# A macaron encoder block in split fp32: six of eight chunk pairs of the up stages by block products, with weight sums on GpSimd and the gated product kept in DRAM

## What is computed

```
def swiglu(h, w_gate, w_up, w_down):
    return (jax.nn.silu(h @ w_gate) * (h @ w_up)) @ w_down

h = swiglu(rmsnorm(x, pre_g), w_gate, w_up, w_down)     # w_gate, w_up 2048 x 5632; w_down 5632 x 2048
x = x + 0.5 * rmsnorm(h, post_g)
```

## Time and profile before

| | us |
|---|---|
| median of 3 runs | 1826.41 (1826.05 to 1826.48) |
| profiled execution, its own time | 1826.47 |
| its span, first to last instruction | 1824.7 |
| TensorE busy | 1799.3 (99%) |
| VectorE busy | 1300.0 (71%) |
| ScalarE busy | 896.5 (49%) |
| GpSimd busy | 53.2 (3%) |
| mean granted clock of TensorE | 0.996 |

### The profile page before, as it was taken

How to read it: one execution, slowest core, us unless ns; L and a number is a source line. 1 busy time by engine, 2 the same in 40 slices (tenths; PEclk the granted TensorE clock), 3 DMA queues, 4 the chain that set the end, 5 groups by cost and what they waited for, 6 DMA issues and landing times.

```text
span 1824.7 us, 20137 instructions
## 1 busy us (share of the span) xinstructions
PE 1799.3 (99%) x8226; PEld 1493.4 (82%) x8226; DVE 1300.0 (71%) x1333; ACT 896.5 (49%) x1003; POOL 53.2 (3%) x111
## 2 busy tenths in 40 slices
PE   7899999999999999999999999999999999999998
PEld 6788888888888888888888887888888888888886
DVE  4788888888865544765754547888889888755544
ACT  3655455455644433654234446545555555644432
POOL 0000000000000000170000000000000000000000
PEclk9999999999999999999999999999999999999999
DMA  7466666666666566665443665666666666665563
GB/s 254 127 196 194 210 196 189 211 200 193 199 211 193 197 193 191 196 186 171 134 142 117 209 194 162 193 210 197 196 197 197 195 198 205 217 193 192 195 196 128
DMA packets 150652, 345.36 MB, mean 189 GB/s; under 512 B 10568, under 2 KB 11152, under 8 KB 150176
## 3 DMA queue, kind: packets, MB, share of 16 engines
q1 hardware_dynamic: 149712, 339.79, 59.2%
q0 software_dynamic: 736, 4.26, 0.7%
q10 hardware_dynamic: 112, 0.03, 0.0%
HBM read 341.94 MB, written 2.10 MB: 189 GB/s over the span
## 4 chain that ended last, share of the span: by engine, by line
PE 95%; DVE 2%; ACT 1%; issue 1%; DMA 0%; DVEq 0%; POOLq 0%; POOL 0%; ACTq 0%
PE ps L1152 25%; PE ps L1154 25%; PE ps L1153 25%; PE ps L1346 5%; PE ps L1348 5%; PE ps L1347 5%; PE ps L1457 1%; PE ps L1301 1%; DVE wlo L716 1%; ACT xT_hi L438 0%; ACT whi L380 0%; PE ps L1494 0%; ACT xT_hi L418 0%; DVE xT_lo L779 0%; PE ps L1286 0%
## 5 line engine op out<-in xcount | busy, mean ns | idle before, releaser
L716 DVE TENSOR_TENSOR wlo<-raw,whi 128x1024 fp32r<-128x1024 f32 x520 | 626.5, 1225 | 345.7 <-ACT whi L380 343.8
L380 ACT ACTIVATE whi<-raw 128x1024 fp32r<-128x1024 f32 x520 | 542.1, 1058 | 526.1 <-DMA raw<-in_ffn_w_down_dram 241.6
L1152 PE MATMUL ps<-whi,xT_hi 128*128 128x512 f32 x1248 | 494.1, 396 | 15.1 <-DVE wlo L716 13.9
L1154 PE MATMUL ps<-whi,xT_lo 128*128 128x512 f32 x1248 | 487.8, 391 | 0.0
L1153 PE MATMUL ps<-wlo,xT_hi 128*128 128x512 f32 x1248 | 487.2, 390 | 0.0
L1152 PE MATMUL ps<-whi,hT_hi 128*128 128x512 f32 x832 | 324.2, 390 | 0.0
L1154 PE MATMUL ps<-whi,hT_lo 128*128 128x512 f32 x832 | 323.8, 389 | 0.0
L1153 PE MATMUL ps<-wlo,hT_hi 128*128 128x512 f32 x832 | 323.7, 389 | 0.0
L1152 PEld LDWEIGHTS ps<-whi,xT_hi 128*128 128x128 f32 x1248 | 235.2, 188 | 68.6 <-issue 17.0
L1154 PEld LDWEIGHTS ps<-whi,xT_lo 128*128 128x128 f32 x1248 | 235.1, 188 | 49.9
L1153 PEld LDWEIGHTS ps<-wlo,xT_hi 128*128 128x128 f32 x1248 | 235.4, 189 | 46.6
(11 more groups left out here) (154 smaller groups left out, 1661.1 us busy)
## 6 DMA issues: line engine op xcount, KB each, us to landing
raw<-in_ffn_w_down_dram SPq DMA_DIRECT2D x176, 512.0 KB, 4.6
raw<-in_ffn_w_gate_dram SPq DMA_DIRECT2D x116, 512.0 KB, 3.7
raw<-in_ffn_w_up_dram SPq DMA_DIRECT2D x116, 512.0 KB, 3.6
raw<-in_w_in_dram SPq DMA_DIRECT2D x80, 512.0 KB, 3.6
raw<-in_w_out_dram SPq DMA_DIRECT2D x32, 512.0 KB, 4.1
srawB<-in_ffn_w_up_dram SPq DMA_DIRECT2D x30, 512.0 KB, 3.8
srawB<-in_ffn_w_gate_dram SPq DMA_DIRECT2D x30, 512.0 KB, 4.7
srawA<-in_ffn_w_up_dram SPq DMA_DIRECT2D x30, 512.0 KB, 3.8
```

The lines of the kernel that those rows point to most:

```text
L380: nc.scalar.activation(whi[:, slot(g), :], raw[:, slot(g), :], ACT.Copy).then_inc(hi_ready, 1)
L716: V.tensor_tensor(wlo[:, slot(g), :], raw[:, slot(g), :], whi[:, slot(g), :].bitcast(f32), ALU.subtract).then_inc(lo_ready, 1)
L1152: mm(bank, a_hi, whi[:, s, c0:c0 + NT], start=start, stop=False, skip_group_check=skip)
L1154: return mm(bank, a_lo, whi[:, s, c0:c0 + NT], start=False, stop=stop, skip_group_check=skip)
```

## The change

- `NS = 6`, `PLAIN = 2`: six pairs of a tile by block products, two plain.
- The four blocks of a pair are loaded into one of two staging buffers `stg`. The sums are made by **GpSimd** (`weight_sums`) from there into one of three areas `sraw` (`area(q) = (q + 1) % 3`). The hi and lo parts of the raw blocks are made from `stg`, those of the sums from `sraw`, with semaphores of their own (`s_bhi`, `s_blo`, `s_thi`, `s_tlo`).
- GpSimd also makes the token sums (`token_sums`, in two parts of three pairs), and in each tile the lo part of one of the four plain halves (`by_pool`, `plain_lo`).
- The ring for plain halves in tiles 1 to 10 has 2 slots (4 before).
- The gated product no longer goes to `hT` in SBUF: SP stores it to DRAM tile by tile (`store_h`) and loads it back in the down stage (`load_h`), where TensorE transposes it (`hidden`) and ScalarE and VectorE make hi and lo straight from PSUM.
- The orders of all engines in `first_tile`, `up_tile`, `up` and `down` are new. In the first FFN's first tile the transposes of x are made one step earlier.

```diff
-PAIRS = (0, 1, 2)
-PLAIN = 5
-NS = len(PAIRS)
+NS = 6
+PLAIN = KC // 2 - NS
...
+RING_ORDER = (6, 5, 2, 3, 7, 0, 1, 4)
...
+def by_pool(g):
+    return any(b + 16 <= g < d and (g - b) % (2 * PLAIN) == 2 for b, d in ((U1, D1), (U2, D2)))
...
 def area(q):
-    return (q + 1) % 2
+    return (q + 1) % 3
...
+    stg = [at("stg0", 22, [P, 4, NT]), at("stg1", 54, [P, 4, NT])]
...
                 def sums(j, s):
                     q = NS * (j - 1) + s
-                    a = area(q)
+                    dst = stg[q % 2]
                     if q >= 2:
-                        sp.wait_ge(p_done, 7 * (NQ * f + q - 1))
-                    elif q == 1:
-                        sp.wait_ge(w_used, b + 12)
+                        sp.wait_ge(s_t, NQ * f + q - 1)
+                        sp.wait_ge(s_blo, NQ * f + q - 1)
+                    else:
+                        sp.wait_ge(w_used, b + 5)
+                    sp.dma_start(dst[:, 0:2, :], part(1, s, j)).then_inc(s_in[q % 2], 16)
+                    sp.dma_start(dst[:, 2:4, :], part(0, s, j)).then_inc(s_in[q % 2], 16)
...
                 for j in range(1, FTILES):
-                    plain(j, 2)
-                    sums(j, 2)
-                    plain(j, 3)
+                    sums(j, 3)
+                    sums(j, 4)
+                    sums(j, 5)
+                    store_h(f, j - 1)
                     if j < FTILES - 1:
                         sums(j + 1, 0)
-                    plain(j, 4)
+                    plain(j, 1)
                     if j < FTILES - 1:
                         sums(j + 1, 1)
+                        sums(j + 1, 2)
                         plain(j + 1, 0)
-                        plain(j + 1, 1)
+
+            def store_h(f, u):
+                sp.wait_ge(h_ok, 2 * (FTILES * f + u + 1))
+                sp.dma_start(h_d[f][u], flat(gated_h[u % 2][:])).then_inc(h_st[u % 2], 16)
+
+            def load_h(f, u):
+                sp.wait_ge(h_st[u % 2], stored(f, u))
+                if u >= 3:
+                    sp.wait_ge(h_tr, 2 * (FTILES * f + u - 1))
+                sp.dma_start(flat(h_back[back(u)][:]), h_d[f][u]).then_inc(h_in[back(u)], 16)
...
+            def weight_sums(f, q):
+
+                w, r = sraw[area(q)], stg[q % 2]
+                pool.wait_ge(s_in[q % 2], 32 * (NQ // 2 * f + q // 2 + 1))
+                if q >= 3:
+                    pool.wait_ge(p_done, 7 * (NQ * f + q - 2))
+                elif q == 1:
+                    pool.wait_ge(w_used, (U2 if f else U1) + 14)
+                link(nc.gpsimd.tensor_tensor(w[:, T3:T1 + 1, :], r[:, 0:1, :].broadcast_to([P, 2, NT]),
+                                             r[:, 1:3, :], ALU.subtract))
+                link(nc.gpsimd.tensor_tensor(w[:, T2, :], r[:, 1, :], w[:, T1, :], ALU.subtract))
+                nc.gpsimd.tensor_tensor(w[:, T4, :], r[:, 3, :], w[:, T2, :], ALU.subtract).then_inc(s_t, 1)
+
+            def plain_lo(b, j):
+
+                g = b + 16 + 2 * PLAIN * j - 2
+                pool.wait_ge(hi_ready, g + 1)
+                nc.gpsimd.tensor_tensor(wlo[:, slot(g), :], raw[:, slot(g), :],
+                                        whi[:, slot(g), :].bitcast(f32), ALU.subtract).then_inc(pool_lo, 1)
+
+            token_sums(0, 0)
+            token_sums(0, 1)
+            weight_sums(0, 0)
             inv_root(1, 0)
+            for q in range(1, NQ):
+                weight_sums(0, q)
+                if q % NS == NS - 1:
+                    plain_lo(U1, q // NS + 1)
...
+            def hidden_hi(f, u):
+
+                if u == 0:
+                    act.wait_ge(p_done, 7 * NQ * (f + 1))
+                    act.wait_ge(post_ok, 8 * (FTILES - 1) * (f + 1))
                 for c in range(2):
-                    act.wait_ge(h_tr, 2 * (FTILES * f + j) + 1 + c)
-                    nc.scalar.activation(flat(hT[:, 4 * j + 2 * c:4 * j + 2 * c + 2, :]), ps[4 + c][:],
-                                         ACT.Copy).then_inc(h_ev, 1)
...
+                    act.wait_ge(h_tr, 2 * (FTILES * f + u) + 1 + c)
+                    nc.scalar.activation(flat(hT_hi[:, 4 * u + 2 * c:4 * u + 2 * c + 2, :]), ps[4 + c][:],
+                                         ACT.Copy).then_inc(h_hi, 1)
```

ScalarE's order in a tile is now: `sum_hi` 2, `block_hi` 3, `plain_hi` 0, `block_hi` 4, `sum_hi` 3, `block_hi` 5, `sum_hi` 4, `sum_hi` 5, `plain_hi` 1, `block_hi` of the next tile's pair 0, the copy `U`, `sum_hi` 0 and `block_hi` 1 and `sum_hi` 1 of the next tile, `silu`, `block_hi` 2 of the next tile. VectorE's and TensorE's:

```diff
             def up_tile(b, j):
                 f = 0 if b == U1 else 1
...
+                last = j == FTILES - 1
+                if j > 1:
+                    gated(b, j - 1)
+                block_lo(f, j, 2)
                 sum_lo(f, j, 2)
-                plain_lo(b, j, 3)
+                block_lo(f, j, 3)
+                plain_lo(b, j, 0)
+                block_lo(f, j, 4)
+                sum_lo(f, j, 3)
+                block_lo(f, j, 5)
+                sum_lo(f, j, 4)
+                sum_lo(f, j, 5)
+                if not last:
+                    block_lo(f, j + 1, 0)
+                lo(b + 16 + 2 * PLAIN * j - 1)
+                if last:
+                    lo(b + UP)
                 combine(f, j)
...
+                    sum_lo(f, j + 1, 0)
+                    block_lo(f, j + 1, 1)
+                    sum_lo(f, j + 1, 1)
...
             def up(b):
                 f = 0 if b == U1 else 1
                 first_tile(b)
                 for j in range(1, FTILES):
-                    for i in range(NS):
-                        plain(b, j, i)
-                        products(f, j, i)
-                    plain(b, j, 3)
-                    hidden(f, j - 1)
-                    plain(b, j, 4)
+                    for s in range(3):
+                        products(f, j, s)
+                    plain(b, j, 0)
+                    for s in range(3, NS):
+                        products(f, j, s)
+                    plain(b, j, 1)
```

More of the change, by code:

```diff
@@ L117, in build @@
     nat = at("nat", 200, [P, TOK, NT])
+    nat1 = at("nat1", 148, [P, TOK, NT])
+    gated_h = [nat, nat1]
+    h_back = [nat1, at("h_odd", 168, [P, TOK, NT]), at("h_even", 172, [P, TOK, NT])]
+    h_d = [nc.dram_tensor(f"gated{f}", (FTILES, P, TOK * NT), f32, kind="Internal").ap() for f in range(2)]
     ident = at("ident", 204, [P, P])
@@ L207, in flat, with block_sum, stored, back @@
             return ap.rearrange("p a b -> p (a b)")
+        def block_sum(ap, part):
+            return ap[:, part].rearrange("p a b c -> p (a b c)")
+        def stored(f, u):
+            return 16 * ((6, 5)[u % 2] * f + u // 2 + 1)
+        def back(u):
+            return 0 if u == 0 else 2 - u % 2
+        def landed(f, u):
+            return 16 * (f + 1 if u == 0 else 5 * f + (u + 1) // 2)
         @block.sync
@@ L323, in load_gain, with token_sums @@
                 pool.dma_start(gpost[:], gain[0:1, :].broadcast_to([P, D])).then_inc(gain_in, 16)
+            def token_sums(f, part):
+                if f:
+                    pool.wait_ge(u_lo, (23, 28)[part])
+                else:
+                    pool.wait_ge(x_lo, 3 * part + 3)
+                k0 = 6 * part
+                if part:
+                    pool.wait_ge(gp, count[0])
+                link(nc.gpsimd.tensor_tensor(xf[:].rearrange("p n c t -> p (n c) t"), xT_hi[:, k0:k0 + 6, :].bitcast(f32),
+                                             xT_lo[:, k0:k0 + 6, :].bitcast(f32), ALU.add))
+                a11, a12, a21, a22 = (xf[:, :, c, t * P:(t + 1) * P] for t in range(TOK) for c in range(2))
+                link(nc.gpsimd.tensor_tensor(Sf[:, part, 0], a21, a22, ALU.add))
+                link(nc.gpsimd.tensor_tensor(Sf[:, part, 1], Sf[:, part, 0], a11, ALU.subtract))
+                nc.gpsimd.tensor_tensor(Sf[:, part, 2], a21, a11, ALU.subtract)
+                link(nc.gpsimd.tensor_tensor(Sf[:, part, 3], a12, Sf[:, part, 1], ALU.subtract))
+                nc.gpsimd.sem_inc(sf_ok, 1)
@@ L366, in _ @@
             inv_root(6, 3, 1, 2)
+            token_sums(1, 0)
+            token_sums(1, 1)
+            weight_sums(1, 0)
             inv_root(7, 4)
+            for q in range(1, NQ):
+                weight_sums(1, q)
+                if q % NS == NS - 1:
+                    plain_lo(U2, q // NS + 1)
             load_gain(D2, g2post_d)
@@ L872, in up @@
+                combine(f, j)
+                if last:
+                    lo(b + UP + 1)
+                    hidden_lo(f, 0)
+                    gated(b, j)
+                    lo(b + UP + 2)
+                    lo(b + UP + 3)
+                    lo(b + UP + 4)
+                else:
+                    sum_lo(f, j + 1, 0)
+                    block_lo(f, j + 1, 1)
+                    sum_lo(f, j + 1, 1)
             def up(b):
@@ L1318, in first_tile @@
                         keep_busy(10)
-                    if not f and m == 1 and i < 7:
-                        transpose_x(i + 1)
-                    if not f and h == 4:
+                        transpose_x(1)
+                    if not f and h == 8:
                         n = VROWS - VEARLY
@@ L1332, in first_tile @@
                     narrow_half(b + h, i, ps[2 * m:2 * m + 2])
```

(31 more changed lines are left out.)

351 lines of the change are left out of this document (172 added, 179 removed).

## The result

The kernel with the change takes **2157.06 us** in the median of 4 runs (2155.38 to 2160.07), the one before 1826.23 (also 4): ratio 1.1814, 95% interval 1.1794 to 1.1834. It is slower, by 331 us.

A forecast was written before the change was run, and what follows sets the result against it. VectorE's two-SBUF-input instructions and GpSimd's SBUF reads were taken to exclude each other, bounding a tile at 57.8 us against 42.4. The sum: 1826.5 + 308 for 20 tiles + 10 for first tiles = 2145 us, range 2040 to 2320.

The forecast's parts named there:

- One of its signs: Sign of being right: VectorE and GpSimd both near 60 us busy per tile in sum, with overlapping records.
- GpSimd's durations: Two-input operations of GpSimd's sums: 2.43 us for 1024 columns, 1.31 for 512, 32.7 us per tile.
- Both ends of the bound: GpSimd's 1024-column operation: low end 1.06 us from the select's slope, high end 3.7 from 0.46 per 128 columns.
- Exclusion: VectorE instructions with two SBUF inputs and GpSimd's that read SBUF block each other for whole instructions; holds add up.
- shared path: SBUF read interface used by VectorE and GpSimd in turn: 54.9 to 60.7 us of holds per tile.
- The tile: One tile of an up stage: 57.8 us against 42.4, +15.4; over 20 tiles +308 us.
- Floor and staging: TensorE needs 39.4 us a tile, floor about 1785 us; loads and sums over two staging buffers stay under TensorE's pace.
- rival (a): No real exclusion for long operations: TensorE stays the bound, tiles of 39.4 to 41 us, 1793 us; chance 0.12.
- net saving: TensorE's matmuls: about 60 us of tile time saved, some 20 back as down-stage transposes, net 41 us.
- (b): Rival: GpSimd waits only at an instruction's start, then shares; 45 to 48 us a tile, 1890 to 1950 us; chance 0.05.
- (d): Rival: low clock makes TensorE late for the chain product to next product; 66 to 75 a tile, 2310 to 2490; chance 0.07.
- 5 us per FFN: First tiles: GpSimd's token sums and first weight sum form a 20 us chain; adds 5 us per FFN, ends 0 and 15.

The follow-up runs named there:

- the probe: A kernel without the computation, running only VectorE and GpSimd operations alone and side by side; GpSimd's two-input 1024 columns took 2338 ns alone.
- fill_writes: The kernel before plus unused GpSimd work, ten memsets of 1024 columns per product pair in tiles 1 to 10 of both up stages: 1826.52 us, ratio 1.0003.
- sums_memset: The changed kernel with GpSimd's three sums of a pair replaced by six memsets of the same places, so results are wrong: 1788.19 us, ratio 0.9782.
- fill_reads: The kernel before plus unused GpSimd work, four two-input additions of 1024 columns per product pair in tiles 1 to 10: 2149.83 us, ratio 1.177.

## Why the prediction was right

It said 2145 us (2040 to 2320), slower with 0.86; 2157 came out, by the mechanism forecast. One of its signs was misjudged: the two engines' records were to sum to near 60 us a tile, and they sum to 102, since each contains its waits.

- **GpSimd's durations**, 2.43 and 1.31 us from the 128-column row, are 2.34 and 1.26 alone. The slope of 2.2 ns per column is 2.10. Both ends of the bound (1.06 and 3.7) were far off. The Trainium skill's GPSIMD Engine Reference (Performance versus the Vector engine) has 4497 ns for 2048 columns; half of it, 2.25, lies 4% under the probe's 2.34.
- **Exclusion**, extrapolated from holds of 0.1 to 0.3 us, holds for 2.1 us too, and as the forecast took it: whole instructions. Of the tile's shared path the probe's durations make 28.0 + 6 x 4.86 + 2.34 = 59.5 us with every fixed part; the tile takes 58.1, and with the columns alone it is 25.6 + 28.0 = 53.6. So the path is in use for at least 92% of the tile. The 57.8 of the forecast was the middle of two such bounds, a choice and not a result; that it came within 0.4 us is partly luck. The Trainium skill's SBUF — State Buffer (Who interferes with whom) says that a VectorE instruction with two SBUF inputs contends with a GpSimd instruction that reads SBUF, and not with one that only writes it: fill_writes (1826.5 against 2149.8) agrees, and the PSUM case of the probe (one SBUF input, 691 ns) was not slowed.
- **The tile**: 57.8 forecast, 58.19 and 58.01 measured; over 20 tiles that is 20 x 15.7 = 314 us for 308.
- **Floor and staging**: 39.4 a tile and 1785 us for a changed kernel that is bound by TensorE; sums_memset has 39.51 and 1788. That kernel is what rival (a) described, at 1793 (its -44 is given no source; the text's own net saving is 41).
- **Rivals (b) and (d)**: fill_reads and the probe leave no room for (b). Of (d) the first half is there, matmuls at 1.2 GHz behind gaps, not the second: the tile is 58 us and not 66 to 75, with TensorE busy for 46 of them, and two tiles with and without the low clock behind the same wait were equally long.

**One step of the sum was wrong**, and others hid it. The text itself says that some 20 us of transposes come back in the down stages, but the sum adds only 20 x (57.8 - 42.4), in which the 42.4 still holds that 1.0 us a tile and the 57.8 does not: 20 us were left out, and with them the same mechanism gives 2165. The other way, the start of the first FFN turned out lighter. That 2145 lies only 12 us off is thus in part luck. The whole of +333.4, by the copies (U) of before and after:

| stretch | before | after | difference |
|---|---|---|---|
| start to the first U | 101.0 | 106.7 | +5.7 |
| nine steps, first FFN | 381.7 | 523.7 | +142.0 |
| last U to the second FFN's first | 696.6 | 732.6 | +36.0 |
| nine steps, second FFN | 381.6 | 522.1 | +140.5 |
| last U to the end | 263.8 | 273.0 | +9.2 |

The 282.5 us of the steps and two more tiles (31.4), one in each FFN, leave 19.5. The products of the second FFN's down stage, before and after (TensorE's instructions on the hi part, first and last start), and, from the waits of the kernel after, the one in it:

```profile
L1152 PE MATMUL ps<-whi,hT_hi x352: 389/389/473, 1576.5 to 1816.1; 128*128 128x512 f32 x176
```

```profile
L1256 PE MATMUL ps<-whi,hT_hi x352: 389/389/628, 1896.6 to 2149.5; 128*128 128x512 f32 x176
```

```profile
PE ps L1256 <- DVE hT_lo L887: 3.2, 1, 3.2
```

252.9 us against 239.6, +13.3 (+14.2 in the first FFN): ten tiles' transposes and a wait of 3 us for the lo part of the gated product, which the forecast had at nothing, at most 2. The plain tile of the second FFN adds 7.9, where 5 were said. The plain tile of the first FFN ends at 62.7 us where it ended at 74.1, 11.4 us less, which the forecast did not see: TensorE waits there for VectorE's lo parts for 5.0 us in all instead of 13.1. The change makes the transposes of x one step earlier there, but also has a new ring order and new loads of x, and no run separates these. Last, the tile of each FFN that is cut at its first and last U: 26.9 us of a tile lay ahead of U and 15.6 behind it; now 44.0 (first FFN) and 44.9 lie ahead of it and 11.5 behind the last, since U stands later in the tile. Together they grew by 13.0 and 13.9 and not by 15.7, 4.5 us less, as the last tile's plain pair waits 0.7 us for combine where others wait 3.4. The sum of all this is 14.2 + 13.3 + 7.9 - 11.4 - 4.5 = 19.5. "5 us per FFN" was thus wrong in both, with opposite signs.
